# Where three short convolutions are turned and computed in a two-layer block, and into which PSUM banks

## The chip, the cores and the metric

The kernel runs on one core of a Trainium2 chip. The metric is the device time of one execution in microseconds (us), the lower the better. On the core, TensorE (PE) multiplies, VectorE (DVE), ScalarE (ACT) and GpSimd (POOL) do elementwise work, and SyncE (SP) issues the loads of the weights. PE writes to PSUM, which has eight banks of 128 x 512 floats.

## The reference, cut to what matters

Two blocks of two layers each work on a sequence of 256 tokens of width 1024. The change lies in the second block alone. A layer of it starts with one wide projection, `h @ w_in`, whose columns are cut into sections; each section feeds something different:

```
proj = h @ w_in      # h: (256, 1024)
dn_q, dn_k, dn_v, dn_z, dn_b, dn_a, sw_q, sw_k, sw_v, gate_a, gate_b = split(proj)
# delta branch: a causal convolution with 4 taps over time, then silu
xp = pad(x, 3 rows ahead);  y = silu(sum(xp[:, j:j + S] * w[j] for j in range(4)))   # x: dn_q, dn_k, dn_v
q = l2norm(q) * 128 ** -0.5;  k = l2norm(k)         # 8 heads of 128
o = gated_delta_rule(q, k, v, g, beta)              # chunks, triangular solves
y_a = (rmsnorm(o) * silu(z)) @ w_up_dn
# window branch: 16 query heads, 2 key heads, window of 128, with a sink
y_b = swa_sink(sw_q, sw_k, sw_v) @ w_up_sw
x = x + rmsnorm((sigmoid(gate_a) * y_a + sigmoid(gate_b) * y_b) @ w_o)
x = x + rmsnorm(square(relu(rmsnorm(x) @ w_ff1)) @ w_ff2)
```

All of it is in fp32; the kernel splits each weight into a high and a low part and makes three matmuls of each product.

## The kernel before

**Pieces.** A section (1024 columns of the projection) is two jobs of 512 columns, here called its halves, as `dq0` and `dq1`. A half accumulates the two blocks of 128 tokens into two PSUM banks: the first half of every section into banks 0 and 1, the second into banks 2 and 3. A half has four pieces, a piece is 12 matmuls of 128 x 512 (L421, L422, L423). For every piece ACT copies the weights' high part (L374, 128 x 1024) some pieces ahead, and DVE subtracts it for the low part (L384). Banks 4 and 5 (`SCORE`), 6 (`TURN`) and 7 (`OUT`) serve the small matmuls.

**The order is written out by hand.** `plan_two` makes a list of steps: after each of a section's eight pieces stand the small steps of that position. I call these positions 0 to 7 of a section. Every engine walks through the same list and issues its share of each step in that order, so each engine has a fixed order of its own, and semaphores tie them together. From `gb` on the sections are run in half pieces, with one list of steps (a slot, made by `delta_slots`) after each half piece: slots 0 to 7 lie in `gb0`, 8 to 15 in `gb1`, 16 to 31 in `ga`.

**Who frees a bank.** PE calls `core.free(pe, bank)` before it writes a bank anew, and waits there for the last reader of what was in it. The first piece of a half does so for both of its banks at once.

**The convolutions.** `dk`, `dq` and `dv` (keys, queries, values) come out of PE with tokens on partitions. ACT evacuates a half (L1841, `conv_in`). A turn step (L445) transposes a quarter of the section, two heads of 128 features, with four transposes into one bank, which gives features on partitions and time along the free axis. DVE then computes the four taps straight from that bank: two multiplies (L2016) and six multiply-adds (L2018), one after the other in place. Its semaphore `convolved` is what frees the bank. `silu` (ACT, L1808, 128 x 2048, with a table load ahead of it and another ahead of the next exponential) waits for all four quarters; `square` (ACT, L1816), `squares` (PE, L1549), a copy of the sums (ACT, L1811), `squares_turn` (PE, L1559) and a power on POOL (L951) then make the norm of q or k.

**The order around them, before.** In section `dk` positions 4 to 7 turn `sk` and `sq`, which need the rotation on POOL (L970). In `dq` positions 0, 2, 4, 6 turn `dk` 0 to 3 into banks 2, 3, 0, 1, and the silu of `dk` is at position 7. In `dv` the same positions turn `dq` 0 to 3 into the same banks, and the norm of `dk` is spread over positions 1, 3, 5 and 7. `dv` 0 to 3 are turned in slots 1, 10, 12 and 17 of the delta stage (banks 2, 0, 1, 2), and the silu and norm of `dq` run in slots 2, 3, 7 and 9. Sections `dq` and `dv` also hold the window attention, one head for each position: scores (L1571, L1573), the maximum (DVE, L937), exponentials (ACT, L1877), a turn (L1581), ACT's copy of it (L1887), and the output (L1589 to L1591), which waits for that copy. The delta stage then inverts triangular matrices by levels (L1654, L1677, L1678, with DVE's L2219 to L2224 between them).

## Time and profile before

| what | value |
|---|---|
| median of 3 runs | 1751.0 us (1748.91 to 1752.21) |
| the profiled execution | 1750.58 us |
| its span, first to last instruction | 1748.8 us |
| mean granted TensorE clock in it | 0.996 of full speed |
| PE / DVE / ACT / POOL busy | 1707.3 / 1170.1 / 922.3 / 212.1 us |

The busy figures are sums over the span. PE has 98% of it, so only little time passes in which PE does nothing. What an edit off PE costs is read from the places where PE waits: a wait of PE adds to the time, other engines' work adds nothing until PE waits for it. The profiled execution is 1.8 us longer than its span.

### The profile page before, as it was taken

How to read it: one execution, taken by the hardware profiler on the slowest of the kernel's cores; microseconds unless marked ns; L12 is line 12 of the kernel's file. 1: busy time of each engine (PE TensorE's matmuls, PEld its weight loads, DVE VectorE, ACT ScalarE, POOL GpSimd, SP SyncE). 2: the span in 40 equal slices, each digit the busy share in tenths (PEclk: the TensorE clock that was granted, in tenths of full speed). 3: DMA queues.
4: the chain of work that ended last, by engine and by line, in shares of the span. 5: the costliest groups of instructions: out<-in, count | busy, mean ns of one | idle time of the engine just before them, and what ended most of it. 6: DMA issues, size and time to landing. Idle time of an engine off the chain costs nothing.

```text
span 1748.8 us, 28216 instructions
## 1 busy us (share of the span) xinstructions
PE 1707.3 (98%) x10753; PEld 1403.6 (80%) x10753; DVE 1170.1 (67%) x2216; ACT 922.3 (53%) x1696; POOL 212.1 (12%) x334
## 2 busy tenths in 40 slices
PE   9999999999999999999999999999999999999998
PEld 7878878888788788877777778888887787878887
DVE  5655667766566676677867776666677867776655
ACT  5355375453554754557545455555567545455553
POOL 1201200022030000311202000000301202000000
PEclk9999999999999999999999999999999999999999
DMA  8543544555444445633333455554633322455552
GB/s 294 166 164 125 169 132 157 188 178 193 140 135 160 137 155 178 219 121 97 121 98 98 146 172 187 185 186 161 216 121 98 120 98 98 146 171 184 185 185 92
DMA packets 137133, 270.10 MB, mean 154 GB/s; under 512 B 5548, under 2 KB 8744, under 8 KB 137000
## 3 DMA queue, kind: packets, MB, share of 16 engines
q1 hardware_dynamic: 134928, 265.44, 45.2%
q10 hardware_dynamic: 2072, 2.86, 0.5%
q8 instruction: 87, 1.43, 0.3%
q14 instruction: 46, 0.38, 0.1%
HBM read 267.23 MB, written 1.05 MB: 153 GB/s over the span
## 4 chain that ended last, share of the span: by engine, by line
PE 83%; DVE 6%; ACT 4%; issue 3%; POOL 3%; DMA 0%; ACTq 0%; DVEq 0%; POOLq 0%
PE bank L421 20%; PE bank L423 20%; PE bank L422 20%; PE bank L402 5%; PE bank L445 3%; PE bank L404 3%; DVE buf L2018 2%; DVE lo L384 1%; POOL scratch L965 1%; PE bank L1677 1%; PE bank L1654 1%; PE bank L607 1%; PE bank L1620 1%; ACT hi L374 1%; DVE buf L2016 1%
## 5 line engine op out<-in xcount | busy, mean ns | idle before, releaser
L421 PE MATMUL bank<-hi,xhl 128*128 128x512 f32 (+1 forms) x1792 | 725.4, 405 | 5.8 <-issue 2.9
L423 PE MATMUL bank<-hi,xhl 128*128 128x512 f32 (+1 forms) x1792 | 698.9, 390 | 0.0
L422 PE MATMUL bank<-lo,xhl 128*128 128x512 f32 (+1 forms) x1792 | 696.5, 389 | 0.0
L374 ACT ACTIVATE hi<-raw 128x1024 fp32r<-128x1024 f32 (+1 forms) x504 | 519.9, 1051 | 235.7 <-PE bank L423 217.4
L384 DVE TENSOR_TENSOR lo<-raw,hi 128x1024 fp32r<-128x1024 f32 (+1 forms) x504 | 606.0, 1220 | 55.1 <-PE bank L423 39.5
L421 PEld LDWEIGHTS bank<-hi,xhl 128*128 128x128 f32 x1792 | 337.5, 188 | 78.8 <-issue 15.3
L423 PEld LDWEIGHTS bank<-hi,xhl 128*128 128x128 f32 x1792 | 336.7, 188 | 73.0
L422 PEld LDWEIGHTS bank<-lo,xhl 128*128 128x128 f32 x1792 | 338.1, 189 | 60.0
L402 PE MATMUL bank<-xhl,hi 128*128 128x512 f32 x384 | 136.0, 398 | 0.0
L404 PE MATMUL bank<-xhl,lo 128*128 128x256 f32 x384 | 107.8, 281 | 0.0
L402 PEld LDWEIGHTS bank<-xhl,hi 128*128 128x128 f32 x384 | 72.1, 188 | 17.8
L445 PE MATMUL bank<-square,buf 128*128 128x128 f32 x472 | 71.2, 274 | 4.1 <-POOL buf L970 2.5
L509 POOL TENSOR_SCALAR small<-small 128x1 f32<-128x1 f32 (+1 forms) x13 | 4.7, 360 | 577.7 <-ACT scratch L502 577.5
L404 PEld LDWEIGHTS bank<-xhl,lo 128*128 128x128 f32 x384 | 72.5, 189 | 0.5
L937 DVE CUSTOM_DVE_ANT_0 scratch<-bank,masks 128x128 f32<-128x128 f32 (+1 forms) x128 | 39.2, 353 | 47.7 <-PE bank L599 24.4
L445 PEld LDWEIGHTS bank<-square,buf 128*128 128x128 f32 x472 | 56.0, 140 | 18.0 <-issue 8.9
L800 DVE TENSOR_SCALAR buf<-bank,small 128x512 f32<-128x512 f32 x48 | 33.8, 746 | 46.4 <-PE bank L423 46.4
L2018 DVE SCALAR_TENSOR_TENSOR buf<-bank,small,buf 128x255 f32<-128x255 f32 (+1 forms) x144 | 62.7, 477 | 2.5
L716 ACT ACTIVATE scratch<-scratch,small 128x128 f32<-128x128 f32 x64 | 28.6, 448 | 57.7 <-DVE small L937 57.7
L2145 DVE TENSOR_TENSOR buf<-bank,buf 128x256 f32<-128x256 f32 x48 | 17.0, 417 | 59.3 <-ACT buf L1861 59.3
L1877 ACT ACTIVATE scratch<-scratch,small 128x128 f32<-128x128 f32 x64 | 28.6, 447 | 34.6 <-DVE small L937 33.6
L1861 ACT ACTIVATE buf<-bank 128x256 f32<-128x256 f32 x48 | 14.6, 389 | 55.8 <-PE bank L404 55.8
(316 smaller groups left out, 1855.2 us busy)
## 6 DMA issues: line engine op xcount, KB each, us to landing
raw<-in_w_in SPq DMA_DIRECT2D x135, 1024.0 KB, 5.1
raw<-in_w_ff SPq DMA_DIRECT2D x64, 1024.0 KB, 5.3
raw<-in_w_proj_a SPq DMA_DIRECT2D x8, 1024.0 KB, 5.1
raw<-in_w_proj_b SPq DMA_DIRECT2D x8, 1024.0 KB, 5.0
raw<-in_w_out SPq DMA_DIRECT2D x8, 1024.0 KB, 5.4
raw<-in_w_up_sw SPq DMA_DIRECT2D x8, 1024.0 KB, 5.0
raw<-in_w_up_dn SPq DMA_DIRECT2D x8, 1024.0 KB, 5.1
raw<-in_w_o SPq DMA_DIRECT2D x8, 1024.0 KB, 5.1
```

Source lines behind the costliest of these rows:

```text
L374: act.activation(self.hi[g % HI_RING][:, 0:w], src, ACT.Copy).then_inc(self.hi_ready, 1)
L384: dve.tensor_tensor(self.lo[g % LO_RING][:, 0:w], src, self.hi[g % HI_RING][:, 0:w].bitcast(F32), ALU.subtract).then_inc(self.lo_ready, 1)
L402: pe.matmul(out, hi, self.xhl[job.xt][:, row, :, :].rearrange("p a t -> p (a t)"), start=first, stop=False, skip_group_check=True)
L404: mm = pe.matmul(out[:, 0:S], lo, xh[:, row, :], start=False, stop=last, skip_group_check=True)
L421: pe.matmul(out, xh[:, row, t], self.hi[slot % HI_RING][:, w], start=first, stop=False)
L422: pe.matmul(out, xh[:, row, t], self.lo[slot % LO_RING][:, w], start=False, stop=False)
L423: mm = pe.matmul(out, xl[:, row, t], self.hi[slot % HI_RING][:, w], start=False, stop=last)
L445: mm = pe.transpose(bank[:, (j * TB + tb) * P:(j * TB + tb + 1) * P], src[:, tb, c:c + P], core.ident)
L716: ins = act.activation(prob[h % 2][:, 0, cols], masked[:, h % 2, cols], ACT.Exp, scale=-1.0, bias=t.negmax[:, h % 2, tb:tb + 1], accum_out ...
L800: ins = dve.tensor_scalar(role[name][:, tb, cols], B[job.banks[tb]][:, :], t.r[:, s.stage, tb:tb + 1], None, ALU.mult)
L937: ins = dve.tensor_tensor_reduce(masked[:, cols], bank[:, cols], core.masks[:, which, keys], -SCALE, -NEG if negsink is None else negsink, ...
L2018: ins_ = dve.scalar_tensor_tensor(y, x, w, y, ALU.mult, ALU.add)
```

## The change

Five things move; no arithmetic is added or taken away, and the number of instructions on PE, DVE, ACT and POOL stays.

1. The four quarters of a convolved section are no longer turned in the next section. The first two, which need only the first half (`dk0`), are turned during the second half's pieces, and the last two at positions 0 and 2 of the next section: `dk` 0 and 1 at positions 4 and 5 of section `dk`; `dk` 2, 3 at 0, 2 of `dq`; `dq` 0, 1 at 5, 7 of `dq`; `dq` 2, 3 at 0, 2 of `dv`; `dv` 0, 1 at 5, 7 of `dv`; `dv` 2, 3 in slots 1 and 5 of the delta stage.
2. Quarter n is turned into bank n, the bank that the section itself has just filled and ACT has read.
3. A turn waits for its own half (`conv_in` of `dk0` or `dk1`), and no longer always for the second.
4. The turns of `sk` and `sq` in section `dk` move one position later, with banks now named in `TURN_BANK`.
5. `silu` and the norm move forward: silu, square and squares of `dk` to positions 3, 4 and 6 of `dq` (its `squares_turn` and `scales` to 0 and 2 of `dv`); those of `dq` to positions 3, 4 and 6 of `dv`, its `squares_turn` to slot 1; the silu of `dv` to slot 10.

```diff
     work = [w[:1] + w[:0:-1] if len(w) == 3 else w for w in attention("s", HEADS)]
+    turn = lambda name, f: [("turn", name, f)]
     p.run(sec("dk", D), [[("rope", "sk", 0), ("rope", "sk", 1), ("rope", "sq", 0)], [("rope", "sq", 1)], [], [],
-                         [("turn", "sk", 0)], turns("sq")[0], turns("sq")[1] + turns("sq")[2], turns("sq")[3] + work[0]])
-    conv = lambda n: [[("turn", n, (0, 2, 4, 6).index(i))] if i in (0, 2, 4, 6) else [] for i in range(8)]
-    p.run(sec("dq", 0), [b + a for a, b in zip(conv("dk"), work[1:9])][:7] + [work[8] + [("silu", "dk")]])
-    norms = [[], [("square", "dk")], [], [("squares", "dk")], [], [("squares_turn", "dk")], [], [("scales",)]]
-    p.run(sec("dv", 2 * D), [c + a + b for a, b, c in zip(work[9:17], conv("dq"), norms)])
+                         turn("dk", 0), turn("sk", 0) + turn("dk", 1), turn("sq", 0) + turn("sq", 1),
+                         turn("sq", 2) + turn("sq", 3) + work[0]])
+    conv = lambda old, new: [turn(old, 2), [], turn(old, 3), [("silu", old)], [], turn(new, 0), [], turn(new, 1)]
+    sums = [[], [], [], [], [("square", "dk")], [], [("squares", "dk")], []]
+    p.run(sec("dq", 0), [c + a + b for a, b, c in zip(work[1:9], conv("dk", "dq"), sums)])
+    norms = [[("squares_turn", "dk")], [], [("scales",)], [], [("square", "dq")], [], [("squares", "dq")], []]
+    p.run(sec("dv", 2 * D), [c + a + b for a, b, c in zip(work[9:17], conv("dq", "dv"), norms)])
...
-    put(2, ("silu", "dq"))
-    put(3, ("square", "dq"))
-    put(7, ("squares", "dq"))
-    put(9, ("squares_turn", "dq"))
+    put(1, ("squares_turn", "dq"))
...
-    put(21, ("silu", "dv"))
-    for at, name, n in ((1, "dv", 0), (10, "dv", 1), (12, "dv", 2), (17, "dv", 3), (21, "kd", 0), (27, "ys", 0),
+    put(10, ("silu", "dv"))
+    for at, name, n in ((1, "dv", 2), (5, "dv", 3), (21, "kd", 0), (27, "ys", 0),
...
-TURN_BANK = {("dv", 0): 2, ("dv", 1): 0, ("dv", 2): 1, ("dv", 3): 2,
+TURN_BANK = {("dv", 0): 0, ("dv", 1): 1, ("dv", 2): 2, ("dv", 3): 3,
+             ("sk", 0): OUT, ("sq", 0): TURN, ("sq", 1): OUT, ("sq", 2): TURN, ("sq", 3): OUT,
...
-                            "dq": ("conv_in", "dq1"), "dk": ("conv_in", "dk1"), "dv": ("conv_in", "dv1"),
+                            "dq": ("conv_in", f"dq{f // 2}"), "dk": ("conv_in", f"dk{f // 2}"), "dv": ("conv_in", f"dv{f // 2}"),
```

**PE, from the last turn of section `dq` to the first piece of `dv0`.** Names: L445 is a turn (four transposes), L421 opens a piece, L1571 scores, L1589 to L1591 outputs, L1581 the attention's turn; in brackets stand the semaphores waited for. Line numbers of the changed kernel are one higher. Before:

```order
L445 MATMUL bank1<-square,buf1 128x128 [waits main_conv_in]
L445 MATMUL bank1<-square,buf1 128x128 x3
L421 MATMUL bank2<-hi1,xhl0 128x512 [waits lo_ready]
...
L1571 MATMUL bank4<-buf8,buf5 128x128 [waits main_sq_copied,main_s_max]
...
L1589 MATMUL bank7<-buf8,scratch 128x64 [waits main_s_copied,main_ys]
L1590 MATMUL bank7<-buf8,scratch 128x64
L1591 MATMUL bank7<-buf8,scratch 128x64
L1581 MATMUL bank6<-square,scratch 128x128 [waits main_s_prob,main_s_copied]
L1581 MATMUL bank6<-square,scratch 128x128 x2
L421 MATMUL bank0<-hi2,xhl0 128x512 [waits lo_ready,main_convolved]
```

After:

```order
L1590 MATMUL bank7<-buf8,scratch 128x64 [waits main_s_copied,main_ys]
L1591 MATMUL bank7<-buf8,scratch 128x64
L1592 MATMUL bank7<-buf8,scratch 128x64
L1582 MATMUL bank6<-square,scratch 128x128 [waits main_s_prob,main_s_copied]
L1582 MATMUL bank6<-square,scratch 128x128 x2
L445 MATMUL bank1<-square,buf0 128x128 [waits main_conv_in]
L445 MATMUL bank1<-square,buf0 128x128 x3
L421 MATMUL bank0<-hi2,xhl0 128x512 [waits lo_ready,main_convolved]
```

Before, a piece and a head of the attention stand between the last turn into bank 1 and the piece that waits for `convolved`; after, nothing does. The order is the same at the end of section `dv`, where `dv` 1 is turned into bank 1 ahead of `gb0`.

**ACT, around the silu of `dk`** (L1808/L1809), which writes buf3; L1816/L1817 is `square`, L1877/L1878 an exponential, L1887/L1888 the copy that the attention's output waits for. Before:

```order
L1887 ACTIVATE scratch<-bank6 128x384 [waits main_s_summed,main_s_turned]
L1808 ACT_TABLE_LOAD
L1808 ACTIVATE buf3<-buf3 128x2048 [waits main_convolved]
L374 ACTIVATE hi0<-raw0 128x1024 [waits pieces_used,unit_loaded0]
L1877 ACT_TABLE_LOAD [waits main_s_turned]
L1877 ACTIVATE scratch,small<-scratch,small 128x128 [waits main_s_max]
L1877 ACTIVATE scratch,small<-scratch,small 128x256
L1881 ACTIVATE small<-small 128x2 [waits main_s_sink]
L1887 ACTIVATE scratch<-bank6 128x384 [waits main_s_summed,main_s_turned]
L374 ACTIVATE hi1<-raw0 128x1024 [waits pieces_used]
L1816 ACTIVATE buf4<-buf3 128x2048 [waits main_silu]
```

After:

```order
L1888 ACTIVATE scratch<-bank6 128x384 [waits main_s_summed,main_s_turned]
L1809 ACT_TABLE_LOAD
L1809 ACTIVATE buf3<-buf3 128x2048 [waits main_convolved]
L374 ACTIVATE hi2<-raw2 128x1024 [waits pieces_used,unit_loaded2]
L1817 ACTIVATE buf4<-buf3 128x2048 [waits main_silu]
L1878 ACT_TABLE_LOAD [waits main_s_turned]
L1878 ACTIVATE scratch,small<-scratch,small 128x128 [waits main_s_max]
L1878 ACTIVATE scratch,small<-scratch,small 128x256
L1882 ACTIVATE small<-small 128x2 [waits main_s_sink]
L1888 ACTIVATE scratch<-bank6 128x384 [waits main_s_summed,main_s_turned]
```

`square` has moved ahead of the table load, the exponentials and the copy of the next head. After the change the same sequence stands once more in section `dv`, for `dq`.

**DVE, in the delta stage, from the end of a convolution in slot 1 to the low parts of `gb1`.** L2191/L2192 multiplies decays by betas, L2197/L2198 scales a gram matrix, L384 is a low part, L2017 and L2019 are the taps. Before:

```order
L2018 SCALAR_TENSOR_TENSOR buf7<-bank2,small,buf7 128x253
L384 TENSOR_TENSOR lo3<-raw0,hi2 128x1024 [waits pieces_used,hi_ready]
L2191 TENSOR_TENSOR buf5<-buf5 128x512 [waits main_betas_copied,main_decay_exp]
L2191 TENSOR_TENSOR scratch<-scratch 128x512 [waits main_betas_copied,main_decay_exp]
L384 TENSOR_TENSOR lo4<-raw0,hi3 128x1024 [waits pieces_used,hi_ready]
L2197 SCALAR_TENSOR_TENSOR buf5<-bank6,small,buf5 128x128 [waits main_decay_beta,main_gram]
...
L2197 SCALAR_TENSOR_TENSOR scratch<-bank4,small,scratch 128x128 [waits main_decay_beta,main_gram]
...
L384 TENSOR_TENSOR lo0<-raw1,hi4 128x1024 [waits pieces_used,hi_ready]
L384 TENSOR_TENSOR lo1<-raw1,hi5 128x1024 [waits pieces_used,hi_ready]
L2212 TENSOR_TENSOR scratch<-narrow,scratch 128x256 [waits main_level_mask] x2
```

After:

```order
L2192 TENSOR_TENSOR buf5<-buf5 128x512 [waits main_betas_copied,main_decay_exp]
L2192 TENSOR_TENSOR scratch<-scratch 128x512 [waits main_betas_copied,main_decay_exp]
L384 TENSOR_TENSOR lo4<-raw0,hi3 128x1024 [waits pieces_used,hi_ready]
L2198 SCALAR_TENSOR_TENSOR buf5<-bank6,small,buf5 128x128 [waits main_decay_beta,main_gram]
...
L2198 SCALAR_TENSOR_TENSOR scratch<-bank4,small,scratch 128x128 [waits main_decay_beta,main_gram]
...
L2017 TENSOR_SCALAR buf7<-bank3,small 128x256 [waits main_turned]
...
L2019 SCALAR_TENSOR_TENSOR buf7<-bank3,small,buf7 128x253
L384 TENSOR_TENSOR lo0<-raw1,hi4 128x1024 [waits pieces_used,hi_ready]
```

The convolution of `dv` 3, into bank 3, now stands directly behind the two gram matrices; `gb1`, which starts three half pieces after that turn, writes banks 2 and 3.

## Rows read from the trace of the kernel before

**Rows 1.** The page, part 1: busy time of PE.
```profile
PE 1707.3 (98%) x10753; PEld 1403.6 (80%) x10753; DVE 1170.1 (67%) x2216; ACT 922.3 (53%) x1696; POOL 212.1 (12%) x334
```

**Rows 2.** PE's waits: engine, line, releaser: us in total, times, longest.
```profile
PE bank L1654 <- DVE buf L2221: 7.7, 4, 2.0
PE bank L1589 <- ACT scratch L1887: 5.3, 5, 1.5
```

**Rows 3.** Timeline, PE: start us, us, [idle before <- releaser]; second block, first layer.
```profile
745.45 0.63 PE L445 MATMUL bank<-square,buf 128*128 128x128 f32 x4 [1.24 <-POOL buf L970]
...
798.25 0.41 PE L1589 MATMUL bank<-buf,scratch 128*128 128x64 f32 x2 [1.47 <-ACT scratch L1887]
...
823.14 0.41 PE L1589 MATMUL bank<-buf,scratch 128*128 128x64 f32 x2 [1.10 <-ACT scratch L1887]
...
828.90 0.47 PE L421 MATMUL bank<-hi,xhl 128*128 128x512 f32 x1 [0.43 <-DVE buf L2018]
...
850.56 0.63 PE L1559 MATMUL bank<-square,scratch 128*128 128x128 f32 x4 [1.38 <-ACT scratch L1811]
...
876.13 0.69 PE L1654 MATMUL bank<-buf 64*64 64x64 f32 x32 [1.84 <-DVE buf L2221]
```

**Rows 4.** Timeline, PE, at the turn of `dk` 3 and the piece behind it.
```profile
783.63 0.60 PE L445 MATMUL bank<-square,buf 128*128 128x128 f32 x4
783.99 0.47 PE L421 MATMUL bank<-hi,xhl 128*128 128x512 f32 x1
...
786.93 0.49 PE L1571 MATMUL bank<-buf 64*128 64x128 f32 x4
```

**Rows 5.** Timeline, DVE: the taps of `dk` 3, and the end of those of `dq` 3.
```profile
784.27 0.88 DVE L2016 TENSOR_SCALAR buf<-bank,small 128x256 f32<-128x256 f32 x2 [0.23 <-PE bank L445]
785.18 2.68 DVE L2018 SCALAR_TENSOR_TENSOR buf<-bank,small,buf 128x255 f32<-128x255 f32 x6
...
826.11 2.69 DVE L2018 SCALAR_TENSOR_TENSOR buf<-bank,small,buf 128x255 f32<-128x255 f32 x6
```

**Rows 6.** Timeline, ACT: table load for the silu, square, and the copy of the sums.
```profile
791.18 1.28 ACT L1808 ACT_TABLE_LOAD   x1
...
798.96 1.91 ACT L1816 ACTIVATE buf<-buf 128x2048 f32<-128x2048 f32 x1
...
807.98 0.60 ACT L1811 ACTIVATE scratch<-bank 128x512 f32<-128x512 f32 x1
```

**Rows 7.** Timeline, POOL: the power of `dk`'s norm.
```profile
819.19 2.91 POOL L951 TENSOR_TENSOR small<-small 128x16 f32<-128x16 f32 x1
```

**Rows 8.** Timeline, DVE, delta stage: taps, low part, decays, second gram.
```profile
834.90 0.87 DVE L2016 TENSOR_SCALAR buf<-bank,small 128x256 f32<-128x256 f32 x2
...
838.40 1.21 DVE L384 TENSOR_TENSOR lo<-raw,hi 128x1024 fp32r<-128x1024 f32 x1
839.54 0.68 DVE L2191 TENSOR_TENSOR buf<-buf 128x512 f32<-128x512 f32 x1
...
845.69 1.12 DVE L2197 SCALAR_TENSOR_TENSOR scratch<-bank,small,scratch 128x128 f32<-128x128 f32 x4
```

**Rows 9.** Timeline, PE, delta stage: the second gram and what follows.
```profile
841.41 1.05 PE L1620 MATMUL bank<-buf 128*128 128x128 f32 x8
842.22 0.47 PE L421 MATMUL bank<-hi,xhl 128*128 128x512 f32 x1
```

**Rows 10.** Windows: stretch, its us, busy of PE, PEld, DVE, ACT, POOL, then PEclk.
```profile
1399.00:1400.00 1.00, 1.00 (x15) 0.88 (x7) 0.89 (x2) 0.67 (x3) 0.65 (x1) 0.50 0.00 0
1474.00:1475.00 1.00, 1.00 (x3) 0.80 (x3) 0.49 (x1) 1.00 (x3) 0.00 (x0) 0.50 0.00 0
```

**Rows 11.** Timeline, PE: behind the level wait, first layer, then second layer.
```profile
878.45 0.40 PE L421 MATMUL bank<-hi,xhl 128*128 128x512 f32 x1
...
1398.20 1.06 PE L1654 MATMUL bank<-buf 64*64 64x64 f32 x32 [1.83 <-DVE buf L2221]
...
1402.09 0.39 PE L421 MATMUL bank<-hi,xhl 128*128 128x512 f32 x1
```

4 rows, old and new, of the table TURN_BANK are left out of this document.

## The prediction, on record before the changed kernel ran

> **What bounds the kernel now.** I read the page's busy shares first: PE is busy for 1707.3 of 1748.8 us [rows 1], so about 41 us are all that waits can give back, and what the change can cost is new waits of PE. Next the list of PE's waits: the largest kinds are L1654 for DVE (7.7 us in 4 waits, up to 2.0) and L1589 for ACT's copy (5.3 us in 5) [rows 2]. Then PE's timeline, which shows where the waits of the second block's first layer stand [rows 3]: 1.24 at the turn of `sq`, 1.47 and 1.10 at outputs of the attention, 0.43 at the start of `gb0`, 1.38 at `squares_turn` of `dq`, 1.84 in the inverse. The second layer repeats them nearly to the hundredth. I take each edit to one of these places, work out one layer, and double.
>
> **What goes away, per layer.** The turn of `sq` comes a piece later, and a piece takes 2.94 us (783.99 to 786.93) [rows 4], more than the 1.24 it waited: −1.24. The wait of 1.10 at 823.14 came from the power on POOL, 2.91 us long [rows 7], which kept a small POOL step of the attention, so ACT's exponential, so the copy. Its `squares_turn` goes to position 0 of `dv`, where DVE will just have finished a convolution that PE waited for, and where a turn and scores stand between it and the next output: I take −1.10, with 0 as the other end. `squares_turn` of `dq` waited for ACT's copy of the sums; now it has a position more: −1.38. At 876.13 PE waited for DVE, which had the taps of `dv` 3 (3.6 us, below) in its queue; those move to slot 5: −1.84. The 0.43 at `gb0` is contained in B below. Sum −5.56.
>
> **What is added, per layer.**
> A. Start of `dv0`. In the order after the change the turn of `dq` 1 into bank 1 stands directly ahead of `dv0`'s first piece, which must have bank 1 free. The taps begin 0.64 us after the turn begins (783.63 to 784.27) and end at 787.86, 4.23 after it [rows 4, 5]; at 828.90 PE went on 0.10 after DVE's end at 828.80 [rows 3, 5]. Without a wait the piece follows the turn after 0.36 (783.63 to 783.99) [rows 4]. So PE loses 4.23 + 0.10 − 0.36 = 3.97. Before, a piece of 2.94 and a head of the attention covered this. Queued behind this wait is all of PE's work, and no other engine has anything for it. DVE's own order adds nothing: the outputs and the reciprocal ahead of the taps are as before at position 6.
> B. Start of `gb0`, the same with `dv` 1: 3.97, in place of 0.43: +3.54.
> C. Start of `gb1`, banks 2 and 3. DVE after the second `rows` step, counted from 834.90 with start-to-start times [rows 8]: a copy 0.1, taps 3.5, low part 1.14, decays 2 x 0.6, low part 1.14, grams 2 x 1.04, taps 3.59, which gives 847.65; PE 0.1 later. The decays no longer wait for ACT, whose silu and square of `dq` have left this stretch. PE: the second gram at 841.41 moves 0.44 later through `squares_turn`, then 0.81 for the gram [rows 9], 0.36 for the turn, 2.94 for a piece: 845.96. Wait 1.8. Ends: 0, if DVE gets through 2 us sooner, and 3.5, if the decays still wait.
> D. `dk`'s silu and square in `dq`. The wait of 1.47 at 798.25 is ACT's chain from the table load at 791.18 (load, silu, high part, load, exponentials, copy). `square`, 1.91 us [rows 6], stood behind that copy and now stands inside the chain, and the turn that lay on PE's side there (0.36) has moved away: 1.47 + 1.9 + 0.36 = 3.7 in place of 1.47. +2.3.
> E. The same sequence for `dq` in `dv`, which in the delta stage cost PE only the 1.38 counted above: +3.7. Ends for D and E: 2 less each, if the exponentials had slack that the trace hides; more only if the next copy is late as well, which the piece after it, 2.94, should cover.
> F. `squares` of `dq` writes bank 7 and the output right behind it needs bank 7 read by ACT: one copy, 0.60 [rows 6], plus hand-over, less nothing: +0.8. `squares` of `dk` goes to bank 6, with an output ahead of the next user: 0.
> Two more edits cost nothing. In section `dk` the taps of `dk` 0 and 1 (7.2 us) have three pieces (8.8 us) and five turns of 0.36 beside them before `dq0` starts, on a DVE that has only low parts there. The silu of `dv` at slot 10 finds ACT with four pieces of high parts in hand.
> Sum 3.97 + 3.54 + 1.8 + 2.3 + 3.7 + 0.8 = 16.1; less 5.56: +10.5 per layer, +21.1 for both. Against the profiled execution's 1750.6 that is 1771.7.
>
> **The clock.** In the second layer two level waits of 1.83 and about 2 us were followed by a granted clock of 0.50 (1.2 GHz in place of 2.4) [rows 10]. In the first layer the same waits were not (878.45 runs on at the usual pace, below), and the mean of 0.996 leaves room for hardly more falls than these two and one at the start. What one fall costs: from the level's matmul to the same L421, 1398.20 to 1402.09 = 3.89 against 876.13 to 878.45 = 2.32 [rows 3, 11], so 1.57. The change makes eight waits of 3.7 to 4.0 us, twice as long as those after which the clock fell half the time; I take it to fall after each. Part of a fall can lie inside the wait, so I take 1.3 each (an estimate; ends 0 and 1.57): 8 x 1.3 = 10.4, less the 1.57 of the fall at 1398, whose wait goes: +8.8. The forecast is 1771.7 + 8.8 = 1780. The profiled execution and the median of the runs (1751.0) differ by 0.4, so this holds for both.
> The Trainium skill's page "TensorE: Matmul & The Clock Gate", in "What's actually happening", says that the throttled state is the default and that activity releases it, and in "Why this matters for your kernels" it advises against idle gaps of PE between bursts of matmuls. By that rule each of the eight waits puts PE back to 1.2 GHz for a while, which the rows above bear out for half of the waits half as long; a reader who lets it out gets 1771.7.
>
> **The rivals.**
> R1, the clock stays up: all waits come, none is followed by a fall, as behind the waits at 798.25 and 876.13. 1771.7, or 1770 without the old fall. It speaks for it that half the 2 us waits left the clock alone; against it, the length. 15%.
> R2, the ACT chains are shorter than I make them (D and E near nothing, because exponentials and copies slip in earlier) and only A, B and C stay: per layer 3.97 + 3.54 + 1.8 + 0.8 − 5.56 = 4.6, 9.1 for both, with four falls 5.2 less 1.57: 1763. 8%.
> R3, faster: one mechanism, at the bank. If the taps of `dq` 1 and `dv` 1 are through before PE comes to the new half, because PE arrives late anyway (an attention step of position 7 that already waits about 4 us for ACT), A and B are no new waits, and the silu chain takes their place or falls within them. Then the edits' removals stand nearly alone: 1750.6 − 11.1 + 2 x 1.8 = 1743. It decides at 4 us of wait ahead of the turn; the trace shows none at position 7, and the rows of the order show nothing between turn and piece. 4%.
> R4, nothing changes: new waits only take the place of the old and the DVE work freed in the delta stage pays the rest; it needs A and B to be 2.8 each in place of about 4, with D to F at nothing and the clock up: 1750. 3%.
> The likeliest, 1780, holds 70%.
>
> **How the numbers follow.** The range reaches from 1766 (R1 with C and one chain at their low ends) to 1793 (every fall at 1.57, C at 3.5, the power's wait of 1.10 still there, and one or two falls more after C). The likeliest case alone has 1774 to 1788. This kernel's runs tell a difference of about 0.2% (3.5 us). Faster by more: 4%. Within it: 3%. Slower by more: 93%.
>
> **What would show it.** PE's waits: L421 for DVE's taps, four of 3.7 or so (A, B, idle counted from the turn's end) and two of 1 to 2 (C); the output for ACT's copy, four of 3 to 3.7 (D, E); no wait for the rotation on POOL, none over 1 us at `squares_turn`, and the level wait at `ga` gone while the later one in `zz` stays. PEclk at 0.50 right after most of the eight. DVE's and ACT's busy sums stay within 1%. The forecast is wrong if the waits for the taps are under 3 us, if the chain's waits stay at 1.5, or if a wait that I have not named is over 2 us.

## The result, and the profile after

| | before | changed |
|---|---|---|
| median | 1750.7 us (1748.9 to 1752.2, 4 runs) | 1788.3 us (1784.9 to 1790.3, 4 runs) |
| ratio | | 1.0213, 95% interval 1.0193 to 1.0233 |
| span of the profiled execution | 1748.8 us | 1788.0 us |
| PE busy / idle in it | 1707.3 / 41.5 us | 1724.1 / 63.9 us |
| mean granted TensorE clock | 0.996 | 0.987 |

The kernel is 37.6 us slower. The two spans differ by 39.2 us, and this splits in two: PE is idle 22.4 us longer, and busy 16.8 us longer with the same 10753 matmuls. The busy line of the page after the change, for comparison with [rows 1]:

```profile
PE 1724.1 (96%) x10753; PEld 1418.4 (79%) x10753; DVE 1169.3 (65%) x2216; ACT 922.7 (52%) x1696; POOL 205.3 (11%) x334
```

DVE and ACT do the same work as before in the same busy time. The list of PE's waits (us in total, times, longest), against [rows 2]:

```profile
PE bank L1590 <- ACT scratch L1888: 18.8, 6, 3.9
PE bank L421 <- DVE buf L2019: 18.2, 6, 3.7
PE bank L1655 <- DVE buf L2222: 4.0, 2, 2.0
...
PE bank L1590 <- ACT scratch L1812: 1.4, 2, 0.7
```

Two kinds make 37.0 us. Of the level wait (L1654 before, L1655 now) only the later one of each layer is left, and the rows for the rotation on POOL and for `squares_turn` are gone from the list. PE's timeline of the same layer as in [rows 3], with the idle time before each row in brackets:

```profile
782.69 0.66 PE L1590 MATMUL bank<-buf,scratch 128*128 128x64 f32 x2 [3.71 <-ACT scratch L1888]
...
801.04 0.47 PE L421 MATMUL bank<-hi,xhl 128*128 128x512 f32 x1 [3.74 <-DVE buf L2019]
...
817.24 0.41 PE L1590 MATMUL bank<-buf,scratch 128*128 128x64 f32 x2 [2.28 <-ACT scratch L1888]
...
835.04 0.66 PE L1590 MATMUL bank<-buf,scratch 128*128 128x64 f32 x2 [3.94 <-ACT scratch L1888]
...
843.36 0.43 PE L1590 MATMUL bank<-buf,scratch 128*128 128x64 f32 x2 [0.72 <-ACT scratch L1812]
...
852.48 0.47 PE L421 MATMUL bank<-hi,xhl 128*128 128x512 f32 x1 [3.74 <-DVE buf L2019]
...
872.49 0.47 PE L421 MATMUL bank<-hi,xhl 128*128 128x512 f32 x1 [1.60 <-DVE buf L2019]
```

In this order they are the prediction's D, A, the power's wait, E, F, B and C. The second layer has the same seven: 3.71, 3.74, 2.28, 2.85, 0.72, 3.73, 1.60. (Ahead of C, two half pieces, 2.94 us, stand between the turn of `dv` 3 and `gb1`, as the prediction's sum has it; the "three" in the section on the change counts `gb1`'s own first one.)

The clock, in windows of the first layer (stretch, its us, busy of PE, PEld, DVE, ACT, POOL, PEclk, DMA share, GB/s):

```profile
770.00:781.00 11.00, 8.98 (x56) 6.96 (x52) 6.86 (x21) 9.61 (x13) 1.17 (x5) 1.00 0.29 97
...
784.00:786.00 2.00, 2.00 (x10) 1.90 (x11) 0.63 (x3) 1.58 (x5) 0.00 (x0) 0.50 0.00 0
...
804.00:806.00 2.00, 2.00 (x10) 1.58 (x8) 0.00 (x0) 0.00 (x0) 0.00 (x0) 0.60 1.00 379
...
835.00:838.00 3.00, 2.96 (x14) 2.99 (x15) 0.36 (x2) 2.58 (x8) 0.00 (x0) 0.50 0.03 5
...
854.00:857.00 3.00, 3.00 (x14) 2.82 (x13) 0.64 (x3) 0.00 (x0) 0.00 (x0) 0.53 0.79 238
```

Behind each of the four waits of 3.7 us or more PE works without a gap at a granted clock at or near 0.50 (1.2 GHz), where it stands at 1.00 (2.4 GHz) ahead of them. The second layer has five such falls, the fifth behind the power's wait of 2.28.

Read in windows of 1 us, the nine falls are of two kinds. Four set in 0.4 to 3.1 us before PE's wait ends (D and E of the first layer, E and B of the second) and stay at the low level about twice as long as the other five, which set in between 0.2 us before the wait's end and 1.2 us behind it. In the wait for E, PE does nothing and the clock already reads 0.50:

```profile
833.00:835.00 2.00, 0.00 (x0) 0.00 (x0) 0.00 (x0) 1.99 (x8) 0.19 (x1) 0.50 0.00 0
```

The mean clock says the same in sum: (1 − 0.987) x 1788.0 / 0.5 = 46 us at the low level, where before it was (1 − 0.996) x 1748.8 / 0.5 = 14.

**The chain of the wait at 817.24**, which the prediction had gone. POOL, DVE and ACT in the changed kernel:

```profile
806.76 2.91 POOL L951 TENSOR_TENSOR small<-small 128x16 f32<-128x16 f32 x1
...
809.92 0.19 POOL L2308 TENSOR_TENSOR small<-small 128x2 f32<-128x2 f32 x1
```

```profile
810.14 0.17 DVE L2172 RECIPROCAL small<-small 128x2 f32<-128x2 f32 x1 [2.96 <-POOL small L2308]
810.23 0.85 DVE L2017 TENSOR_SCALAR buf<-bank,small 128x256 f32<-128x256 f32 x2
811.12 2.68 DVE L2019 SCALAR_TENSOR_TENSOR buf<-bank,small,buf 128x255 f32<-128x255 f32 x6
813.72 1.22 DVE L384 TENSOR_TENSOR lo<-raw,hi 128x1024 fp32r<-128x1024 f32 x1
814.85 0.35 DVE L937 CUSTOM_DVE_ANT_0 scratch<-bank,masks,small 128x128 f32<-128x128 f32 x1
```

```profile
815.65 0.40 ACT L1878 ACTIVATE scratch<-scratch,small 128x128 f32<-128x128 f32 x1 [4.13 <-DVE small L937]
...
816.63 0.47 ACT L1888 ACTIVATE scratch<-bank 128x384 f32<-128x384 f32 x1
```

The power keeps POOL, POOL's small step behind it keeps DVE's reciprocal (idle 2.96), and behind the reciprocal DVE has the taps of `dq` 2, a low part and only then the maximum for which ACT's exponential waits; ACT's copy at 816.63 releases PE at 817.24. The trace of the kernel before already has the first half of this chain, behind its power at 819.19:

```profile
822.58 0.17 DVE L2171 RECIPROCAL small<-small 128x2 f32<-128x2 f32 x1 [3.00 <-POOL small L2307]
```

There a low part alone stood between this reciprocal and the next maximum.

### The profile page after: what moved, and what is told of

It reads as the page before. It is cut to its first block, busy times and chain, and to the rows that moved or that the text cites. A ratio compares the mean times of both kernels' runs of the same rounds, so it can differ in the third digit from the quotient of the medians.

```text
span 1788.0 us, 28216 instructions
## 1 busy us (share of the span) xinstructions
PE 1724.1 (96%) x10753; PEld 1418.4 (79%) x10753; DVE 1169.3 (65%) x2216; ACT 922.7 (52%) x1696; POOL 205.3 (11%) x334
## 4 chain that ended last, share of the span: by engine, by line
PE 86%; DVE 6%; ACT 4%; issue 2%; POOL 1%; DMA 0%; ACTq 0%; DVEq 0%; POOLq 0%
PE bank L421 21%; PE bank L423 20%; PE bank L422 20%; PE bank L402 5%; PE bank L445 3%; PE bank L404 3%; DVE buf L2019 2%; DVE lo L384 1%; PE bank L1678 1%; PE bank L1655 1%; PE bank L1621 1%; PE bank L607 1%; DVE buf L2017 1%; POOL small L951 1%; ACT scratch L1932 0%
## 5 line engine op out<-in xcount | busy, mean ns | idle before, releaser
L421 PE MATMUL bank<-hi,xhl 128*128 128x512 f32 (+1 forms) x1792 | 729.5, 407 | 22.5 <-DVE buf L2019 18.2
L384 DVE TENSOR_TENSOR lo<-raw,hi 128x1024 fp32r<-128x1024 f32 (+1 forms) x504 | 604.5, 1218 | 60.7 <-PE bank L423 42.1
L421 PEld LDWEIGHTS bank<-hi,xhl 128*128 128x128 f32 x1792 | 340.0, 190 | 96.2 <-DVE buf L2019 19.8
L445 PE MATMUL bank<-square,buf 128*128 128x128 f32 x472 | 72.6, 280 | 1.6 <-DVE buf L2268 1.5
L445 PEld LDWEIGHTS bank<-square,buf 128*128 128x128 f32 x472 | 58.0, 144 | 14.3 <-issue 5.6
L2019 DVE SCALAR_TENSOR_TENSOR buf<-bank,small,buf 128x255 f32<-128x255 f32 (+1 forms) x144 | 62.7, 477 | 2.5
L716 ACT ACTIVATE scratch<-scratch,small 128x128 f32<-128x128 f32 x64 | 28.6, 448 | 57.8 <-DVE small L937 57.8
L1878 ACT ACTIVATE scratch<-scratch,small 128x128 f32<-128x128 f32 x64 | 28.5, 447 | 40.5 <-DVE small L937 40.2
```

What stands on the lines that cost most here:

```text
L384: dve.tensor_tensor(self.lo[g % LO_RING][:, 0:w], src, self.hi[g % HI_RING][:, 0:w].bitcast(F32), ALU.subtract).then_inc(self.lo_ready, 1)
L421: pe.matmul(out, xh[:, row, t], self.hi[slot % HI_RING][:, w], start=first, stop=False)
L445: mm = pe.transpose(bank[:, (j * TB + tb) * P:(j * TB + tb + 1) * P], src[:, tb, c:c + P], core.ident)
L716: ins = act.activation(prob[h % 2][:, 0, cols], masked[:, h % 2, cols], ACT.Exp, scale=-1.0, bias=t.negmax[:, h % 2, tb:tb + 1], accum_out ...
L2019: ins_ = dve.scalar_tensor_tensor(y, x, w, y, ALU.mult, ALU.add)
```

## The experiments

Every experiment is timed beside the kernel before on the same chip. The table lists all of them; ratios are to the kernel before, with 95% intervals, and idle is span less PE busy of the profiled execution.

| run | median us | ratio | PE busy / idle us | clock |
|---|---|---|---|---|
| the changed kernel | 1788.3 | 1.0213 (1.0193 to 1.0233) | 1724.1 / 63.9 | 0.987 |
| e1 new turns one position earlier | 1764.6 | 1.0081 (1.0064 to 1.0098) | 1717.4 / 45.8 | 0.989 |
| e2 silus and norms back | 1771.6 | 1.0123 (1.0107 to 1.0139) | 1715.2 / 53.2 | 0.988 |
| e3 both | 1753.6 | 1.0008 (0.9996 to 1.0020) | 1706.7 / 41.5 | 0.996 |
| e4 waits filled, 28 matmuls | 1793.2 | 1.0249 (1.0234 to 1.0265) | 1761.1 / 30.4 | 0.998 |
| e5 waits filled, 16 matmuls | 1773.1 | 1.0128 (1.0114 to 1.0142) | 1739.9 / 30.8 | 0.997 |
| e6 taps ahead of the attention | 1787.6 | 1.0206 (1.0188 to 1.0224) | 1721.8 / 63.3 | 0.985 |
| e7 other bank, same order | 1775.3 | 1.0140 (1.0126 to 1.0154) | 1717.8 / 54.5 | 0.990 |
| e8 composed | 1747.2 | 0.9983 (0.9974 to 0.9992) | 1707.6 / 37.8 | 0.996 |
| e9 composed, two places changed | 1735.8 | 0.9912 (0.9898 to 0.9927) | 1704.3 / 28.6 | 0.999 |
| e10 square behind the copy | 1776.5 | 1.0142 (1.0125 to 1.0159) | 1716.5 / 57.8 | 0.988 |

### e1: the new turns one position earlier

```diff
-    conv = lambda old, new: [turn(old, 2), [], turn(old, 3), [("silu", old)], [], turn(new, 0), [], turn(new, 1)]
+    conv = lambda old, new: [turn(old, 2), [], turn(old, 3), [("silu", old)], turn(new, 0), [], turn(new, 1), []]
```

> The changed kernel with the two new turns of a section at positions 4 and 6 in place of 5 and 7, so that a piece and an attention head stand again between the turn into bank 1 and the first piece of the next section. Theory (the convolution is exposed at dv0 and gb0, nothing else): the four waits of 3.74 us on the taps fall to under 0.6 each, PE's idle time drops by about 14 us and some 8 us of clock falls go with them: 1765 us (1762 to 1769). Rival (DVE is short of time in these sections, so the waits come back at another place, behind the maximum or the low parts): over 1778 us, with a new wait on DVE of 2 us or more.

Measured: 1764.6 us. The waits A and B are gone from the list:

```profile
PE bank L1590 <- ACT scratch L1888: 15.7, 6, 3.3
...
PE bank L421 <- DVE buf L2019: 3.2, 2, 1.6
```

L421's waits for the taps fall from 18.2 to 3.2 us, and the 3.2 left are C. The edit does a little more than that: the waits for ACT's copy fall from 18.8 to 15.7, with D at 3.27 in both layers and E at 2.26 and 2.29. Of the 18.1 us less idle, 15.0 are A and B. Two turns a piece earlier are worth 23.7 of the 37.6 us.

### e2: silus and norms at their old places

Turns and banks as in the changed kernel. The silu of `dk` goes back to position 7 of `dq` in the lines left out.

```diff
...
-    norms = [[("squares_turn", "dk")], [], [("scales",)], [], [("square", "dq")], [], [("squares", "dq")], []]
+    norms = [[], [("square", "dk")], [], [("squares", "dk")], [], [("squares_turn", "dk")], [], [("scales",)]]
...
-    put(1, ("squares_turn", "dq"))
+    put(2, ("silu", "dq"))
+    put(3, ("square", "dq"))
+    put(7, ("squares", "dq"))
+    put(9, ("squares_turn", "dq"))
```

> The changed kernel with its turns and banks, but silu, square, squares and squares_turn of dk and dq at their places of before. Theory (ACT's chain of silu, square and exponentials is what adds the waits on ACT's copy): the 3.7 and 3.9 us waits on the copy go back to one of 1.5 us per layer and the 2.28 to 1.1; in return gb1 waits about 4 us for the taps of dv 3 in place of 1.6, since ACT's silu and square of dq hold up the decays ahead of those taps, and 1.4 us at squares_turn of dq come back: about 9 us less idle, with some clock falls less 1774 us (1769 to 1778). Rival (square is off the path and the waits come from the turns' positions): within 3 us of 1788.

Measured: 1771.6 us, 16.7 less than the changed kernel. D, E and F are gone:

```profile
PE bank L421 <- DVE buf L2021: 22.4, 6, 3.8
PE bank L1584 <- ACT scratch L1890: 4.4, 2, 2.2
```

The taps' waits are 4.2 us more than in the changed kernel: C has grown, since DVE's decays again wait for ACT behind the silu and square of `dq`. The wait of 2.2 is the power's again, `squares_turn` now at position 5 of `dv`; two things came otherwise than expected: this wait, which was to go back to 1.1, and the 1.4 at `squares_turn` of `dq`, which did not come back.

### e3: both edits undone

e1 and e2 together; what stays of the change is the banks, the earlier first turns, the later turns of `sk` and `sq`, and the slots of `dv` 2, `dv` 3 and the silu of `dv`.

> Both edits of the two runs before at once: turns at positions 4 and 6, norms at the places of before. Theory (the two causes add up): the exposed taps of dv0 and gb0 and the long chains are gone, rotation and level waits stay gone, gb1 waits about 4 us: 1752 us (1747 to 1757). Rival (they overlap, each fills the wait of the other): over 1762 us.

Measured: 1753.6 us, no difference that can be told. Alone the two edits give 23.7 and 16.7 us, together 34.7, so they overlap by 5.7. C is no part of that, since it is 3.75 in e2 and here alike. What overlaps is mainly E, which e1 alone already cuts from 3.94 to 2.26 and from 2.85 to 2.29, and the old waits of 1.47 at the copy and 0.42 at `gb0`: they are back here, while e2, with A and B in front of them, does not show them. C with the norms back, DVE, then PE:

```profile
842.47 0.69 DVE L2194 TENSOR_TENSOR scratch<-scratch 128x512 f32<-128x512 f32 x1 [2.68 <-ACT scratch L1895]
```

```profile
849.97 0.47 PE L421 MATMUL bank<-hi,xhl 128*128 128x512 f32 x1 [3.75 <-DVE buf L2021]
```

DVE stands 2.68 us for ACT at the decays, the case that the prediction had as C's upper end (3.5).

### e4 and e5: the waits filled with matmuls

Dummy matmuls of 128 x 128, whose results nobody reads, are put where PE would stand, so that PE does not go idle: ahead of the pieces A and B and of the outputs that D and E delay; those for the power's wait stand one position ahead of it, at position 1 of `dv`. The rest of the kernel is the changed one.

```diff
+    for i, n in ((6, 16), (14, 16), (10, 9)):
+        work[i] = work[i][:1] + [("fill", n)] + work[i][1:]
...
-    conv = lambda old, new: [turn(old, 2), [], turn(old, 3), [("silu", old)], [], turn(new, 0), [], turn(new, 1)]
+    conv = lambda old, new: [turn(old, 2), [], turn(old, 3), [("silu", old)], [], turn(new, 0), [], turn(new, 1) + [("fill", 16)]]
...
+                if kind == "fill":
+                    core.free(pe, OUT)
+                    for _ in range(arg):
+                        pe.matmul(B[OUT][:, 0:P], core.ident, core.ones, start=True, stop=True)
```

e4 had 28, 28 and 16 in place of 16, 16 and 9.

> The changed kernel with matmuls of 128 x 128 whose result nobody reads put into its long waits: 28 ahead of each wait for taps at dv0 and gb0, 28 ahead of the outputs that wait for ACT's copy behind the silu, 16 at the wait of 2.28 us. They add no work to the path as long as they are shorter than the wait. Theory (about 17 us of the loss are falls of the granted clock after the waits): most falls vanish, PE's time in the usual matmuls goes back to what it was before the change, 1773 us (1770 to 1778). Rival (the falls cost nothing, since they lie inside the waits, and PE's longer busy time is bookkeeping): 1785 us or more.

Measured for e4: 1793.2 us at a clock of 0.998. It decides nothing, because the fillers were sized wrongly: 28 of them (the trace has two rows for each) ran 6.4 us where 3.7 were to be filled.

```profile
795.82 6.42 PE L1582 MATMUL bank<-square 128*128 128x128 f32 x56
```

> As the filled waits before, but with 16, 16 and 9 matmuls (0.22 us each in the run before, where 28 of them took 6.2 us and overran waits of 3.7), so that they end within the waits; their results are not read. Theory (the falls of the clock after the waits cost about 15 us, the waits themselves the rest): granted clock at 0.996 or above, 1773 us (1770 to 1777). Rival (the falls cost next to nothing, and the 1793 us of the run before were not its overrun): 1785 us or more.

Measured for e5: 1773.1 us, clock 0.997. Now the fillers are no longer than the waits. At A, E and the power 0.16 to 0.29 us of idle are left. At D and B none is seen, but PE comes from the output before to the one or the piece behind the wait in the same time as in the changed kernel: 773.26 to 781.69 against 774.26 to 782.69 at D, 9.10 against 9.12 at B. So they lengthen nothing, and the chains on DVE and ACT are those of the changed kernel. Two windows behind the waits D and B, which the changed kernel runs at 0.50 or near it:

```profile
784.00:786.00 2.00, 2.00 (x11) 1.36 (x9) 1.93 (x5) 0.80 (x1) 0.00 (x0) 1.00 0.00 0
...
846.00:849.00 3.00, 3.00 (x22) 2.61 (x21) 1.42 (x5) 0.00 (x0) 0.00 (x0) 1.00 0.64 183
```

The clock falls cost 1788.3 − 1773.1 = 15.3 us of the 37.6 (the unrounded medians), the waits themselves 22.3.

### e6: the taps ahead of the attention at position 0 of `dv`

```diff
-    p.run(sec("dv", 2 * D), [c + a + b for a, b, c in zip(work[9:17], conv("dq", "dv"), norms)])
+    p.run(sec("dv", 2 * D), [c + (b + a if i == 0 else a + b) for i, (a, b, c) in enumerate(zip(work[9:17], conv("dq", "dv"), norms))])
```

> The changed kernel with one step pair swapped: at position 0 of section dv the turn of dq 2 stands ahead of the attention's steps, so DVE does its taps before the reciprocal that waits for POOL, which is busy with the power of dk's norm. Theory (the wait of 2.28 us at position 1 comes from power, then reciprocal, then taps, then maximum in DVE's order): that wait falls under 0.8 in both layers, 1784 us (1782 to 1787), and no other wait grows by more than 0.5. Rival (POOL's late small step reaches PE through ACT's exponential alone, as I had it in the prediction): the wait stays above 2, time within 1.5 us of the changed kernel.

Measured: 1787.6 us, and the wait of 2.28 has become two:

```profile
808.68 0.49 PE L1572 MATMUL bank<-buf 64*128 64x128 f32 x4 [0.68 <-DVE small L937]
...
810.21 0.41 PE L1590 MATMUL bank<-buf,scratch 128*128 128x64 f32 x2 [0.60 <-ACT scratch L1888]
```

With the taps out from between reciprocal and maximum, 2.28 becomes 1.28, so the rival's "stays above 2" is out, and the order on DVE is shown to be worth 1.0 us of the wait. What is left no longer comes from the power: POOL stands idle for DVE's maximum, which now has the taps ahead of it.

```profile
808.68 0.29 POOL L2302 TENSOR_SCALAR small<-small 128x2 f32<-128x2 f32 x1 [1.23 <-DVE small L937]
```

The wait did not fall under 0.8, and the time, which was to be 1784 us, cannot be told from the changed kernel's. The clock does not fall behind the two short waits, but E of the second layer is 3.76 in place of 2.85, against the expectation that no other wait grows, and PE is idle 63.3 us against 63.9.

### e7: the same order, another bank

```diff
-TURN_BANK = {("dv", 0): 0, ("dv", 1): 1, ("dv", 2): 2, ("dv", 3): 3,
+TURN_BANK = {("dv", 0): 0, ("dv", 1): 2, ("dv", 2): 3, ("dv", 3): 2,
...
-             ("dq", 0): 0, ("dq", 1): 1, ("dq", 2): 2, ("dq", 3): 3}
+             ("dq", 0): 0, ("dq", 1): 2, ("dq", 2): 3, ("dq", 3): 2}
```

> The changed kernel with the order as it is, but dq 1 and dv 1 turned at position 7 into bank 2 (which ACT has just read) in place of bank 1, and quarters 2 and 3 into banks 3 and 2. Theory (it is the bank, which the next half writes first, that exposes the taps at dv0 and gb0): the four waits of 3.74 on the taps vanish as in the run with earlier turns, 1766 us (1762 to 1770). Rival (it is the position: three convolutions now come within three positions, and DVE passes its lag on to the maximum, the output or the start of dv1): waits of 2 us or more on DVE elsewhere, 1775 us or more.

Measured: 1775.3 us. Both theories hold in part: `dv0` and `gb0` no longer wait, but DVE is as late as it was, and part of it shows elsewhere, 1.07 us at the next turn of the attention, 0.76 at `squares_turn` of `dq`, and 2.2 in place of 1.6 at `gb1`:

```profile
PE bank L421 <- DVE buf L2019: 4.4, 2, 2.2
...
PE bank L1582 <- DVE small L2066: 2.1, 2, 1.1
```

The bank gives back 13.1 us, the earlier position 23.7.

This run also shows what a fall of the clock does to the next wait. The power's wait is 2.40 in its first layer, with no fall behind it, and E is 3.95; in the second it is 2.42, the clock stands at 0.56 from 1347 to 1350, and E is 2.69.

### e10: the square behind the copy

```diff
-    sums = [[], [], [], [], [("square", "dk")], [], [("squares", "dk")], []]
+    sums = [[], [], [], [], [], [("square", "dk")], [], [("squares", "dk")]]
...
-    norms = [[("squares_turn", "dk")], [], [("scales",)], [], [("square", "dq")], [], [("squares", "dq")], []]
+    norms = [[("squares_turn", "dk")], [], [("scales",)], [], [], [("square", "dq")], [], [("squares", "dq")]]
```

> The changed kernel with one thing moved: dk's and dq's squares are taken on ScalarE one position later, behind the copy that TensorE waits for, and the sums of squares are multiplied one position later. Theory (the copy waits behind the square of 1.9 us in ScalarE's order, and the square is in the chain of the waits of 3.71 and 3.94 us): each becomes about 1.8 us, 4 x 1.9 = 7.6 us less idle, and about 3 us less of clock falls: 1777 us (1773 to 1781). Rival (the copy waits for its own input, not for the square): the waits stay over 3 us and the time within 3 us of 1788 us.

Measured: 1776.5 us. ACT in the changed kernel, then in e10:

```profile
775.12 1.92 ACT L1809 ACTIVATE buf<-buf 128x2048 f32<-128x2048 f32 x1
776.95 1.04 ACT L374 ACTIVATE hi<-raw 128x1024 fp32r<-128x1024 f32 x1
777.89 1.89 ACT L1817 ACTIVATE buf<-buf 128x2048 f32<-128x2048 f32 x1
779.80 1.28 ACT L1878 ACT_TABLE_LOAD   x1
...
782.08 0.47 ACT L1888 ACTIVATE scratch<-bank 128x384 f32<-128x384 f32 x1
```

```profile
775.89 1.04 ACT L374 ACTIVATE hi<-raw 128x1024 fp32r<-128x1024 f32 x1
776.95 1.28 ACT L1878 ACT_TABLE_LOAD   x1
...
779.23 0.47 ACT L1888 ACTIVATE scratch<-bank 128x384 f32<-128x384 f32 x1
...
780.55 1.90 ACT L1817 ACTIVATE buf<-buf 128x2048 f32<-128x2048 f32 x1
```

With the square behind the copy, D is 1.91 in place of 3.71, and E 0.91 and 0.92. The clock falls here behind the power's wait in both layers, in the changed kernel in the second alone; so E's like is the 2.85 of that layer, and the step from 2.85 to 0.92 is the square's 1.9. F grows to 1.65, its cause not tried. The sum of idle falls by 6.1 us and PE's busy time by another 7.6, together the 11.9 us of the time within 2. So the shorter waits also brought fewer and shorter falls (eight in the second block, two of them of the longer kind, against nine and four), worth as much as the waits themselves.

### e8 and e9: what is left when each wait is taken away

e8 takes the banks and the early first turns of the change, one position earlier than there, and the silus and norms of before; `squares_turn` of `dk` stands behind the attention of position 6 of `dv`, that of `dq` in slot 12, `dv` 3 in slot 10 in bank 0. e9 changes two of its places:

```diff
-    put(12, ("squares_turn", "dq"))
+    put(10, ("squares_turn", "dq"))
...
+SUMS_BANK = {"dk": 0, "dq": OUT}
...
-                    b = SQUARES_BANK[arg]
+                    b = SUMS_BANK[arg]
```

> A version put together from what helped: turns at positions 4 and 6 with their own banks, norms of dk and dq at the places of before except that squares_turn of dk comes behind the attention steps of position 6 of dv (POOL's power then has no small step of the attention behind it that matters) and squares_turn of dq in slot 12; dv 2 in slot 1 into bank 2, dv 3 in slot 10 into bank 0, silu of dv in slot 21. Theory (each wait goes with its cause): of the waits of the kernel before there stay 1.47 at the copy and 0.4 at gb0 in each layer; gone are the rotation's 1.24, the power's 1.1, the 1.38 at squares_turn and the 1.84 of the level, 5.6 per layer, and one clock fall: 1739 us (1736 to 1743). Rival (the waits move on to the next late thing): 1747 us or more.

Measured for e8: 1747.2 us, where the theory had 1739 and the rival 1747 or more: the waits did move on. It has two waits of its own, of which the larger is at the level, behind the power on POOL (PE, then POOL):

```profile
863.48 1.13 PE L1658 MATMUL bank<-buf 64*64 64x64 f32 x32 [2.89 <-POOL buf L2338]
```

```profile
858.25 3.74 POOL L951 TENSOR_TENSOR small<-small 128x16 f32<-128x16 f32 x1
861.96 1.26 POOL L2338 TENSOR_TENSOR buf<-scratch,narrow 128x512 f32<-128x512 f32 x1
```

> The kernel of e8_composed with two of its places changed: the sums of dq's squares are turned in slot 10 of the level, ahead of dv3's turn, and dk's sums of squares are turned in bank 0 in place of bank 6. Theory: the two waits that e8 had new (2.89 us for GpSimd's power of dq at the level, 1.05 us for ScalarE's copy out of bank 6, in each layer) go, and with the first of them the clock falls behind it: 2 x (2.89 + 1.05) = 7.9 us of idle, and up to 2 x 1.3 us of clock, so about 1737 us (1734 to 1741), 0.993 of the kernel before. Rival: VectorE and GpSimd are late at the level whatever stands first, and the waits only move on to dv3's turn or the level's mask: 1744 us or more, with waits of over 2 us in the level.

Measured for e9: 1735.8 us, 0.9912 of the kernel before. Both waits are gone, and nothing of 0.5 us or more took their place; the list begins

```profile
PE bank L1659 <- DVE buf L2226: 4.0, 2, 2.0
PE bank L1594 <- ACT scratch L1892: 3.3, 4, 1.5
```

Against the kernel before, idle is 12.9 us less and busy 3.0 less. Of the first, 11.1 are the rotation's, the power's, `squares_turn`'s and one level wait, 2 x (1.24 + 1.10 + 1.38 + 1.84) by [rows 3], all gone at once, and 1.3 are L421's waits for the taps, those at `gb0` above all. The idea of the change, to turn the first half early, holds, with a piece between DVE's taps and the bank's next use, and ACT's silu where it was. e8 and e9 show these together, not each by itself.

## Why the prediction was right, and where its sizes were off

The sign, the mechanism and the place of each large wait came as forecast; 1788.3 lies inside the range, 8.3 us above the forecast of 1780. Against its own execution (1788.0 + 1.8 = 1789.8 us, 39.2 more than before) the sum had 21.1 + 8.8 = 29.9. Of the 9.3 missing, 1.3 are idle time and 8.0 PE's longer busy time, nearly all the clock's (e5 gives the clock 15.3 us against the 16.8). That the idle time came out so near is in part luck: one term was 4.6 us too low and others some 3 too high.

- A and B, the bank that is turned into right ahead of the piece that needs it: 3.97 predicted, 3.74 measured, in both layers. e1 takes them away and little else. The step from order to wait needed nothing but the length of the taps and the piece that no longer covered them.
- C: 1.8 predicted, 1.60 measured. The claim that the decays no longer wait for ACT is shown by e2 and e3, where they do and C is 3.75, a little above the 3.5 of the upper end.
- D and E: 3.7 each predicted; D 3.71 in both layers, E 3.94 and 2.85. e10 shows that the square in ACT's order was the added part. In the second layer the clock fell behind the power's wait in front of E, and a slower PE meets a shorter wait: from the power's wait to E's, the wait itself left out, PE takes 15.32 us there and 13.86 in the first layer. The two layers of e7 have the same pair with and without the fall (2.69 and 3.95), and e10, with the fall in both, has 0.91 and 0.92. Filling the power's wait alone was not tried.
- F: 0.8 predicted, 0.72 measured.
- The rotation, the `squares_turn` of `dq` and the first level wait: gone, as predicted.
- **The step that failed: the power on POOL, −1.10 per layer.** Measured +1.18, a wait of 2.28, so 2 x 2.28 = 4.6 us of idle where none was left in the sum. The prediction followed POOL's output to ACT alone, and gave the step "DVE will just have finished a convolution" as cover. In the order, DVE's reciprocal waits for POOL too, and the taps of `dq` 2 and a low part stand between it and the maximum. e6 shows it, for 1.0 of the 2.28; the high end that the prediction had kept for this (0, the wait of 1.10 still there) was too low as well. The prediction's own sign of being wrong, an unnamed wait of over 2 us, is touched here: it had named this wait only as one that goes. A, B, C and F were 0.1 to 0.2 too high each and E of the second layer 0.85, some 2 us together, and small waits elsewhere are about 1 us less, so that the sum of idle came out only 1.3 short.
- **The term that was mis-sized: the clock, +8.8.** Measured: 16.8 us more PE busy, and 15.3 us by e5. It fell nine times, not eight, the ninth behind the power's wait in the second layer; and one fall cost 15.3 / 9 = 1.7 us on average, above the 1.57 that I had taken as its upper end from one fall [rows 3, 11]. Some lasted longer than others, the four that set in earliest in the wait. From D to A, the wait for A left out, PE takes 14.61 us with the longer fall behind D and 13.14 in e10 with a short one, for the same work: the longer one costs 1.5 us more. That the clock falls behind each of the eight waits was right, and R1 (clock stays up, 1771.7) is refuted by the changed kernel and measured by e5 at 1773.1: the waits alone were sized to within 2 us.
- The Trainium skill's "TensorE: Matmul & The Clock Gate" ("Why this matters for your kernels") advises against idle gaps of PE between bursts of matmuls. The trace agrees: all eight waits of 2.85 us and more brought a fall here. So did one of 2.28 in the second layer (mean clock 0.64 and 0.67 in the two windows behind it), while that of 2.28 in the first did not:

```profile
818.00:820.00 2.00, 2.00 (x14) 1.79 (x14) 1.63 (x8) 1.38 (x7) 0.44 (x2) 1.00 0.67 153
...
1358.00:1360.00 2.00, 2.00 (x14) 2.00 (x14) 1.59 (x11) 1.38 (x4) 0.44 (x2) 0.64 0.36 48
1360.00:1363.00 3.00, 3.00 (x11) 2.42 (x11) 2.67 (x7) 1.66 (x5) 0.00 (x0) 0.67 0.83 317
```

- R2 (ACT's chains short) falls with D and E; R3 and R4 needed A and B to be hidden, which nothing did.

What stays open: why the clock falls early in some waits and only at the end of others or behind it, and why the same wait of 2.28 brought a fall in one layer and none in the other.

## What to carry to other kernels

When a step is moved into a bank, count what stands between it and the next write of that bank on the engine that waits: a piece of 2.94 us and a head of the attention, or nothing, was here the difference between 0.4 us at most and 3.7, four times. When a step on a side engine is moved, follow every engine that waits for it through that engine's own order; the one that was left out (POOL to DVE's reciprocal, with 3.5 us of taps queued behind it) is the wait that the sum missed. And where TensorE is the bound, price a wait together with its clock: here waits of some 22 us more brought 15 us more of slow matmuls.

## What the runs showed of the hardware that was not expected

- Matmuls without any use made the kernel faster: 16 dummies in a wait of 3.7 us kept the granted clock at 1.00 and gave back 15.3 us in all (e5), while 28 of them overran the wait and cost it again (e4).
- Waits much shorter than those can bring a fall, but not always: of 1.91 us in both layers of e10, and of 1.47 in the first layer of e8 (797.32, the clock at 0.50 from 799 to 801), while the same wait of 1.47 in the kernel before [rows 3] brought none.
- The same power on POOL (128 x 16) took 2.91 us in the kernel before and the changed one, and 3.74 to 3.76 us for `dq` in e2, e3 and e8. In these three DVE ran low parts beside it, in the kernel before and the changed one the taps, another step or nothing; that this is the cause was not tried.
